# A fused two-block transformer on one Trainium2 core: taps of the long convolution over two more gate units, its norm's later links ahead of the splits, the short convolution's branch ahead of the long one's

## The reference

```
h = rms_norm(x);  parts = split(h @ w_in)
ya = rms_norm(diff_attention(...))              # branch 0
yf = forgetting_attention(...)                  # branch 1
yc = silu(layer_norm(conv31(c_a * sigmoid(c_g)) + b))   # branch 2, the long convolution
ys = s_b * conv3(s_c * s_x)                     # branch 3, the short convolution
proj  = einsum('bsnc,ncd->bsnd', stack([ya, yf, yc, ys]), w_branch)
gates = sigmoid(h @ w_gate + b_gate)            # one gate for each branch
mixed = sum_n(gates * proj) @ w_out;  x = x + rms_norm(mixed)
```

## Time and profile before

| | |
|---|---|
| median of 3 runs | 1330.28 us (1328.29 to 1332.39) |
| profiled execution | 1330.64 us, its span 1328.5 us |
| PE busy | 1282.4 us (97%) |
| DVE busy | 838.8 us (63%) |
| ACT busy | 672.4 us (51%) |
| DMA | 211.32 MB, mean 159 GB/s |

### The profile page before, as it was taken

The page is one execution under the profiler, slowest core; times in us unless marked ns, Lnnn a source line. Parts: engine busy times, 40 slices in busy tenths (PEclk is TensorE's granted clock), DMA queues, the critical chain, the costliest instruction groups (busy, mean ns, idle before and its releaser), DMA issues.

```text
span 1328.5 us, 22392 instructions
## 1 busy us (share of the span) xinstructions
PE 1282.4 (97%) x9224; PEld 1201.5 (90%) x9224; DVE 838.8 (63%) x1129; ACT 672.4 (51%) x925; POOL 57.7 (4%) x101
## 2 busy tenths in 40 slices
PE   5999998999999999999999999899999998999997
PEld 5999997999999998899999999888999987999996
DVE  4874447655555655655555589986556566766664
ACT  4874656544445454444444554645354445654552
POOL 4000002000000000100000000010000010000000
PEclk8999999999999999999999999899999999999999
DMA  7750104555554644455654655444556642555550
GB/s 238 203 164 28 64 1 156 193 191 188 189 189 159 206 159 159 147 187 189 189 189 158 211 171 159 128 127 128 159 152 198 190 157 68 177 189 189 189 189 32
DMA packets 160465, 211.32 MB, mean 159 GB/s; under 512 B 5541, under 2 KB 143219, under 8 KB 160387
## 3 DMA queue, kind: packets, MB, share of 16 engines
q1 hardware_dynamic: 157299, 202.77, 48.0%
q0 software_dynamic: 2048, 7.37, 1.6%
q10 hardware_dynamic: 1040, 0.07, 0.1%
HBM read 209.14 MB, written 1.05 MB: 158 GB/s over the span
## 4 chain that ended last, share of the span: by engine, by line
PE 80%; DVE 11%; ACT 4%; issue 2%; DMA 2%; POOL 1%; DVEq 0%; SPq 0%; POOLq 0%; ACTq 0%
PE bank L306 23%; PE bank L309 23%; PE bank L310 23%; PE bank L1173 5%; DVE wlo L300 3%; DVE common L2198 2%; ACT whi L292 1%; PE bank L1662 1%; PE bank L1180 1%; ACT common L544 1%; DVE xlo L615 1%; DMA raw<-in_dn_w_in 1%; PE bank L2218 1%; PE bank L1744 1%; PE bank L1785 1%
## 5 line engine op out<-in xcount | busy, mean ns | idle before, releaser
L300 DVE TENSOR_TENSOR wlo<-raw,whi 128x2048 fp32r<-128x2048 f32 x191 | 437.1, 2291 | 248.4 <-ACT whi L292 248.0
L306 PE MATMUL bank<-xhi,whi 128*128 128x256 f32 x1824 | 523.5, 287 | 12.3 <-DVE xlo L615 11.4
L309 PE MATMUL bank<-xlo,whi 128*128 128x256 f32 x1824 | 516.9, 283 | 0.0
L310 PE MATMUL bank<-xhi,wlo 128*128 128x256 f32 x1824 | 516.9, 283 | 0.0
L292 ACT ACTIVATE whi<-raw 128x2048 fp32r<-128x2048 f32 x191 | 364.4, 1910 | 176.4 <-PE bank L306 107.2
L306 PEld LDWEIGHTS bank<-xhi,whi 128*128 128x128 f32 x1824 | 350.9, 192 | 18.1 <-issue 13.8
L309 PEld LDWEIGHTS bank<-xlo,whi 128*128 128x128 f32 x1824 | 350.8, 192 | 2.6 <-issue 1.0
L310 PEld LDWEIGHTS bank<-xhi,wlo 128*128 128x128 f32 x1824 | 350.6, 192 | 0.0
L306 PE MATMUL bank<-whi,hhi 128*128 128x512 f32 x392 | 154.0, 393 | 3.4 <-DVE hlo L2647 2.5
L309 PE MATMUL bank<-wlo,hhi 128*128 128x512 f32 x392 | 153.7, 392 | 0.0
L310 PE MATMUL bank<-whi,hlo 128*128 128x512 f32 x392 | 153.1, 390 | 0.0
(11 more groups left out here) (318 smaller groups left out, 1572.5 us busy)
## 6 DMA issues: line engine op xcount, KB each, us to landing
raw<-in_mlp_w_up SPq DMA_DIRECT2D x32, 1024.0 KB, 5.4
raw<-in_mlp_w_down SPq DMA_DIRECT2D x32, 1024.0 KB, 5.0
raw<-in_w_in SPq DMA_DIRECT2D x22, 1024.0 KB, 5.3
raw<-in_w_up SPq DMA_DIRECT2D x22, 1024.0 KB, 5.1
raw<-in_dn_w_in SPq DMA_DIRECT2D x16, 1024.0 KB, 6.1
raw<-in_w_gate SPq DMA_DIRECT2D x16, 1024.0 KB, 5.7
raw<-in_mb_w_in SPq DMA_DIRECT2D x12, 1024.0 KB, 5.1
raw<-in_w_down SPq DMA_DIRECT2D x11, 1024.0 KB, 4.8
```

The lines of the kernel that those rows point to most:

```text
L300: nc.vector.tensor_tensor(wlo[:, s, :], raw[:, V % RAW, :], f32(whi[:, s, :]), ALU.subtract).then_inc(lo_ready, 1)
L306: ins = pe.matmul(o, shi, mhi, start=first, stop=False, skip_group_check=True)
L309: pe.matmul(o, shi, mlo, start=False, stop=False, skip_group_check=True)
L310: return pe.matmul(o, slo, mhi, start=False, stop=last, skip_group_check=True)
```

## The change

Three things. `LN` goes from 27 to 29, and the taps are spread over 24 steps (4 to 27) instead of 22 (4 to 25). In DVE's order `dve_norm` and `dve_lo` go ahead of `split_lo` of their steps, now 34 and 35. In the branch units of half 1 branch 3 (short convolution) is multiplied, and taken up by DVE, ahead of branch 2 (long convolution). The banks of the norm are taken where their steps now are.

```diff
-            LN = MIX + 5
+            LN = MIX + 7
...
-            quota = [9, 9, 9, 9, 7, 7] + [0, 8, 10] + [2, 4, 8] + [2, 4, 8] + [2, 5, 8] + [3, 3, 4, 3]
+            quota = [7, 7, 7, 7, 5, 5] + [0, 7, 9] + [1, 4, 8] + [1, 4, 8] + [2, 4, 7] + [5, 6, 5, 5, 5, 5]
...
-            for item in order:
+
+            def norm_bank():
                 if len(S) in (LN + 1, LN + 3, LN + 5):
                     ln.append(bank().use())
+
+            for item in order:
+                norm_bank()
...
                 for g in (2, 3):
+                    norm_bank()
                     gate_at[len(S)] = (j, g)
...
+            BRANCHES = [(0, 1), (1, 0)]
+
             def dve_branches(dve, e):
                 j, b = branch_at[e]
                 uses = S[e].uses
-                for c in range(2):
+                for place, c in enumerate(BRANCHES[b]):
                     n = 2 * b + c
+                    p_ = 2 * b + place
...
-                        for c in range(2):
+                        for c in BRANCHES[half]:
                             n = 2 * half + c
...
                             gemm_features(pe, b.U, b.uses[c], bhi[:, 4 * n:4 * n + 4, :], blo[:, 4 * n:4 * n + 4, :],
-                                          kts=4, wk0=4 * c, begins=(c == 0))
+                                          kts=4, wk0=4 * c, begins=(c == BRANCHES[half][0]))
...
+                    if e == LN + 5:
+                        dve_norm(dve)
+                    elif e == LN + 6:
+                        dve_lo(dve)
                     split_lo(dve, b.U)
...
                     if e == LN + 3:
                         dve_var(dve)
-                    elif e == LN + 5:
-                        dve_norm(dve)
-                    elif e == LN + 6:
-                        dve_lo(dve)
```

More of the change, by code:

```diff
@@ L2380, in dve_branches @@
                     dve.wait_ge(gate.freed, gate.n + 1)
-                    if n == 0:
+                    if p_ == 0:
                         nc.vector.tensor_tensor(macc[j], uses[c].ps[:, :], sg_, ALU.mult).then_inc(uses[c].freed, 1)
@@ L2385, in dve_branches @@
                     dve.wait_ge(uses[c].freed, uses[c].n + 1)
-                    if n == 1:
+                    if p_ == 1:
                         dve.wait_ge(uses[0].freed, uses[0].n + 1)
                     else:
-                        dve.wait_ge(prods[j][n - 2].sem, prods[j][n - 2].value)
-                    nc.vector.tensor_tensor(macc[j], macc[j], sg_, ALU.add).then_inc(prods[j][n - 1].sem, 1)
+                        dve.wait_ge(prods[j][p_ - 2].sem, prods[j][p_ - 2].value)
+                    nc.vector.tensor_tensor(macc[j], macc[j], sg_, ALU.add).then_inc(prods[j][p_ - 1].sem, 1)
             def pe_f(pe):
```

## The result

The changed kernel took 1325.09 us (median of 5 runs, 1322.48 to 1325.76) against 1332.16 us for the kernel before (5 runs, 1328.29 to 1333.24): ratio 0.9948, 95% interval 0.9928 to 0.9967. Timed again later, in twelve runs (experiment 12), the changed kernel took 1326.81 us, ratio 0.9965 (0.9947 to 0.9983). The profiled execution took 1324.67 us, its span 1322.6.

A forecast was written before the change was run, and what follows sets the result against it. DVE was taken to bound the stage's first half, PE the second. 4.65 us around step 15 plus 0.47 at step 35 made 5.1 us off, so 1325.1 us for a median; range 1322.3 to 1329.0.

The forecast's parts named there:

- The first rival: Whole kernel: the forecast itself, 1325.1 us, own range 1324.0 to 1326.5; chance 0.48.
- Lead at L1679: First head's L1679 on DVE, step 13: would begin at 824.7 us instead of 827.19 through fewer early taps.
- The gate at step 9's bank: Short convolution's product at step 9 waits for PE's bank, leaving at most 0.9 us of lead from earlier taps.
- Waits: PE's two waits at step 14's end: 3.25 us falls to some 0.3, the second becomes 0.8 to 1.3.
- Clock: PE behind step 14: clock stays at its upper level, 16 matmuls save 0.09 us each, 1.5 us.
- The second rival: Around step 15: PE's clock still falls, the 1.5 us is lost, 1326.6 us; chance 0.20.
- Step 35: PE's 0.47 us wait for a bank at step 35 goes, since the norm chain moves to gate steps; gain 0.5 us.
- Late taps cost nothing: Steps 22 to 27: added taps are hidden by DVE's waits before splits and by three units of stock; 0 us.
- The margin at the mean: Behind step 29: last tap ends at about 946.6 us, `pe_mean` stands at about 957.6, 11 us of margin.
- So it moves with PE: Second head's pause, 0.81 us at 862.40, stays: DVE's work from 849.6 starts from POOL's root of PE's values; 0 us.
- So no wait is removed: Step 36: the old order had 7 us of slack, so putting the short branch first gives and costs nothing.
- the 0.5 us for the links ahead of the splits: Steps 34 and 35: norm's later links before the splits, ending PE's wait at step 35; gain 0.5 us.

The follow-up runs named there:

- experiment 12: The changed kernel, unedited, timed again on the same chip as experiment 11: 1326.81 us, ratio 0.9965 to the kernel before.
- experiment 3: Changed kernel, but of its 15 early taps only the ten of steps 4 to 8 moved: 1328.5 us, one execution.
- experiment 4: Changed kernel, but of its 15 early taps only the five of steps 9, 11, 12 and 13 moved: 1324.74 us, one execution.
- experiment 11: Changed kernel with ten more taps late, 4 taps instead of 8 in step 15, steps 16 and 19 to 21 adjusted: 1324.5 us, ratio 0.9940 to the kernel before.
- experiment 9: Changed kernel with 4 taps instead of 8 in step 15, the others moved behind step 22: 1324.83 us, one execution.
- experiment 10: Changed kernel with 12 taps instead of 8 in step 15, taken from steps 22 to 27: 1328.72 us, one execution.
- experiment 1: Changed kernel with the norm's late links behind the splits and the long branch first again: 1335.93 us, ratio 1.0027 to the kernel before.
- experiment 5: Changed kernel with only the branch order undone, long convolution first again: 1322.44 us, one execution.
- experiment 6: Changed kernel with only the links' order undone, the norm's two late links behind the splits again: 1329.01 us, one execution.
- experiment 8: Changed kernel with ten more taps moved from steps 9 to 13 into steps 22 to 27: 1324.89 us, ratio 0.9955 to the kernel before.

## Why the prediction was right

Forecast 1325.1 us, measured 1325.09. That the two agree to 0.01 us is luck: the kernel before was taken at 1330.28 us, the median of its first 3 runs, and measured 1332.16 beside the changed one, so the medians differ by 7.1 us where 5.2 was forecast; on the second timing the ratio of 0.9965 makes 4.7 us. The sound comparison is that of the stage, 5.1 us forecast and 4.86 measured. The first rival, that is the forecast's own case, came true, and its steps can be checked one by one.

- *Lead at L1679*: forecast 53.70 less 2.5, measured less 2.47. The gate at step 9's bank was right (experiment 3: 0.89 for a forecast 0.9), and so was the worth of each tap behind it (experiment 4: 1.62 for 1.6). A like gate that the prediction didn't name stands at step 8, whose product waits 1.03 us in the changed kernel; it takes lead that step 9's would have taken, so the sum is the same.
- *Waits*: 0.3 and 0.8 to 1.3 forecast, 0.38 and 1.17 measured; PE at step 15 3.13 us earlier for 2.9 + 0.25 (2.88 of waiting, 0.25 of transposes).
- *Clock*: 1.5 forecast, 1.52 measured. The second rival, that it still falls, can't be called far off: with 1.24 us for 0.38 it did fall (experiment 4). That rival would have given 1326.6.
- *Step 35*: the wait of 0.47 is gone, as forecast. Behind step 18 the stage gained 0.78: the first matmul of step 35 came 0.76 us after the last of step 34 (989.17 and 989.93) and comes 0.12 after it now, which is 0.64. Behind a pause the second matmul comes 0.19 instead of 0.12 us after the first, and this is gone at steps 34 and 35: the other 0.14.
- *Late taps cost nothing*: right, and 42 instead of 31 still cost nothing (experiment 11). The margin at the mean was not the 11 us stated but 9.4, from the last tap's end at 942.98 to `pe_mean` at 952.38: the 957.6 of the text held the time of the mean itself.

Two statements were wrong, and in the sum they were small or cancelled; a third number only looks like a miss.

- "So it moves with PE", of the second head's pause: PE came 4.65 us earlier at step 16, and POOL began L1831 4.65 us earlier too, but ended it only 4.07 earlier, as it now fell into DVE's taps. 0.57 us; experiments 9 and 10 show it.
- "So no wait is removed", of the short branch first, and the 0.5 us for the links ahead of the splits: both compare the new kernel with the old one only. Within the change the later norm steps and the two orders are not independent: the first alone costs 4.5 us and the clock (experiment 1), and the links' order takes that back (experiment 5). The numbers for it were at hand but not put together: the old low half ended at 988.58, 16.6 us behind the begin of step 32 (971.94), two steps of norm later that is 16.6 us behind step 34's, and the long branch, if first, is needed 11.5 behind it.
- The profile's 5.9 us looks like more than the forecast 5.1. It is not: the stage gave 4.86, and 1.5 us are a low clock in the cross attention that the one trace has and the other hasn't.

Not settled: why that stretch falls to the lower clock in one execution and not in another. It fell in six of the fourteen traces of this case (the kernel before, experiments 1, 6, 8, 9 and 10), behind the same pause of 1.7 us in all of them. The part behind the stage took 261.6 to 262.1 us in these six and 258.9 to 260.5 in the other eight. So the 1.5 us can't be credited to the change: experiment 9 differs from the changed kernel by four taps and has it.

## What to carry to other kernels

Where work is spread over a list of steps, look for the place where a downstream consumer first runs dry, and count in full only what stands between it and the last wait ahead of it. Here ten instructions ahead of such a wait were worth 0.9 us, four behind it 1.6. Before moving a chain along the list, write its end and its first reader as distances from the step's begin, for each edit alone and not only for all of them together.

Where the whole time scatters by as much as the effect, compare distances between two marks inside one stage. Here step 15 came 62.03 to 62.05 us behind step 5 in eight traces, and the stage took 288.08 or 288.09 us in three, while the changed kernel's whole time varied from 1322.48 to 1330.05.

## What the hardware showed that was not expected

- A small GpSimd instruction (128x4) took 0.19 us alone and up to 2.35 us when it began within a run of VectorE instructions with two inputs in SBUF; it ended 0.05 or 0.06 us behind the run's last, for 8 and 12 of them alike.
- TensorE's lower clock level came with pauses of 1.24 and 1.17 us with three transposes between them, for 3.4 us, and did not come with 0.38 and 1.17. The clock alone made that longer pause 1.26 us dearer. Yet a single pause of 1.70 us in steady matmuls (experiment 6) left the clock up.
